# Attention scores from split queries and keys in a hybrid attention and state-space block

## The reference, cut to what matters

```python
h = rms_norm(x, norm_mix_pre[l])
z = h @ w_in[l]                       # q | k | v | u | gates
q = partial_rope(q, pos); k = partial_rope(k, pos)
s = jnp.einsum('bnqhgd,bnkhd->bnhgqk', qb, kb).astype(jnp.float32) / math.sqrt(HEAD_DIM)
s = jnp.where(mask[None, :, None, None], s, jnp.finfo(jnp.float32).min)
p = jax.nn.softmax(jnp.concatenate([s, sink], axis=-1), axis=-1)[..., :-1]
o = jnp.einsum('bnhgqk,bnkhd->bnqhgd', p.astype(v.dtype), vb)
...                                   # state-space branch from u, lam, b_re, b_im, c_re, c_im
mixed = (g_attn * y_attn + g_ssm * y_ssm) @ w_out[l]
x = x + rms_norm(mixed, norm_mix_post[l])
a = jax.nn.relu(rms_norm(x, norm_mlp_pre[l]) @ w_up[l])
x = x + rms_norm((a * a) @ w_down[l], norm_mlp_post[l])
```

## Time and profile before

| | |
|---|---|
| median of 3 runs | 2510.0 us (2509.37 to 2514.89) |
| the profiled execution: its time | 2509.61 us |
| its span, first to last instruction | 2507.6 us |
| PE busy | 2483.1 us, 99% |
| DVE busy | 1281.0 us, 51% |
| ACT busy | 683.4 us, 27% |
| POOL busy | 176.3 us, 7% |
| mean granted TensorE clock | 0.998 of full speed |

### The profile page before, as it was taken

The page is one execution under the profiler, slowest core; times in us unless marked ns, Lnnn a source line. Parts: engine busy times, 40 slices in busy tenths (PEclk is TensorE's granted clock), DMA queues, the critical chain, the costliest instruction groups (busy, mean ns, idle before and its releaser), DMA issues.

```text
span 2507.6 us, 30373 instructions
## 1 busy us (share of the span) xinstructions
PE 2483.1 (99%) x11747; PEld 2027.9 (81%) x11747; DVE 1281.0 (51%) x1622; ACT 683.4 (27%) x903; POOL 176.3 (7%) x284
## 2 busy tenths in 40 slices
PE   9999999999999999999999999999999999999998
PEld 7866887877888888888888888888888888888886
DVE  7876688887434442354444344344334434433446
ACT  5145223333422222252222222212212222121222
POOL 1120243430000000000000000000000000000000
PEclk9999999999999999999999999999999999999999
DMA  6431343443334453343332332223332222333342
GB/s 218 111 105 51 101 123 113 125 125 112 118 101 142 142 181 105 102 163 106 101 101 88 105 100 92 84 100 100 100 100 95 89 94 91 99 100 100 100 153 98
DMA packets 83592, 278.22 MB, mean 111 GB/s; under 512 B 17984, under 2 KB 18048, under 8 KB 81728
## 3 DMA queue, kind: packets, MB, share of 16 engines
q1 hardware_dynamic: 64224, 232.81, 28.9%
q0 software_dynamic: 6624, 27.07, 3.3%
q10 hardware_dynamic: 12672, 17.34, 2.0%
HBM read 258.24 MB, written 18.94 MB: 111 GB/s over the span
## 4 chain that ended last, share of the span: by engine, by line
PE 95%; DVE 2%; ACT 1%; DMA 1%; issue 0%; DVEq 0%; POOL 0%; ACTq 0%
PE main L1568 15%; PE main L1570 14%; PE main L1569 14%; PE side L1764 6%; PE side L1763 6%; PE side L1762 6%; PE main L1763 5%; PE main L1764 5%; PE main L1762 5%; PE side L1568 5%; PE side L1570 5%; PE side L1569 5%; PE side L1626 1%; PE side L1707 1%; PE side L1636 1%; PE side L1676 1%
## 5 line engine op out<-in xcount | busy, mean ns | idle before, releaser
L505 ACT ACTIVATE w_hi<-w_raw 128x1024 fp32r<-128x1024 f32 x436 | 453.7, 1056 | 1080.2 <-PE main L1570 396.4
L880 DVE TENSOR_TENSOR w_lo<-w_raw,w_hi 128x1024 fp32r<-128x1024 f32 x436 | 530.7, 1234 | 361.8 <-ACT w_hi L505 342.5
L1568 PE MATMUL main<-h_hi,w_hi 128*128 128x512 f32 x1280 | 505.4, 395 | 2.5 <-DVE h_lo L896 2.5
L1570 PE MATMUL main<-h_hi,w_lo 128*128 128x512 f32 x1280 | 498.9, 390 | 0.0
L1569 PE MATMUL main<-h_lo,w_hi 128*128 128x512 f32 x1280 | 498.6, 389 | 0.0
L1568 PEld LDWEIGHTS main<-h_hi,w_hi 128*128 128x128 f32 x1280 | 240.6, 188 | 57.3 <-issue 6.6
L1570 PEld LDWEIGHTS main<-h_hi,w_lo 128*128 128x128 f32 x1280 | 240.4, 188 | 50.8
L1569 PEld LDWEIGHTS main<-h_lo,w_hi 128*128 128x128 f32 x1280 | 240.7, 188 | 48.1 <-issue 0.2
L1568 PE MATMUL side<-h_hi,w_hi 128*128 128x512 f32 x512 | 199.2, 389 | 0.0
L1569 PE MATMUL side<-h_lo,w_hi 128*128 128x512 f32 x512 | 199.2, 389 | 0.0
L1570 PE MATMUL side<-h_hi,w_lo 128*128 128x512 f32 x512 | 199.2, 389 | 0.0
(11 more groups left out here) (322 smaller groups left out, 3135.2 us busy)
## 6 DMA issues: line engine op xcount, KB each, us to landing
w_raw<-wstream SPq DMA_DIRECT2D x436, 512.0 KB, 3.6
gate_scratch<-gate_stage ACTq DMA_DIRECT2D x16, 512.0 KB, 3.9
gate_attn<-gate_scratch POOLq DMA_DIRECT2D x8, 512.0 KB, 3.7
gate_ssm<-gate_scratch POOLq DMA_DIRECT2D x8, 512.0 KB, 4.5
x_rows<-x_rows POOLq DMA_DIRECT2D x4, 1024.0 KB, 11.5
x_scratch<-x_rows ACTq DMA_DIRECT2D x4, 1024.0 KB, 4.0
x_all<-x_scratch POOLq DMA_DIRECT2D x4, 1024.0 KB, 8.1
x<-x_t POOLq DMA_DIRECT2D x7, 512.0 KB, 5.9
```

Of the source, the lines that this page charges most:

```text
L505: nc.scalar.activation(WH[:, s], RAW[:, s], ACT.Copy).then_inc(hi_ready, 1)
L880: tt(WL[:, s], RAW[:, s], WH[:, s].bitcast(F32), ALU.subtract).then_inc(lo_ready, 1)
L1568: mm(o, wh, xh[:, k0 + k], start=first and k == 0, stop=False)
L1570: ins = mm(o, wl, xh[:, k0 + k], start=False, stop=last and k == 3)
```

## The change

The scores are made as three products of halves in fp32r, as the units are: high queries by high keys, low queries by high keys, high queries by low keys, all into the same bank. For that ACT writes `q_hi` (four pieces of 128x1024, behind units 12, 13, 16, 20) and `k_hi` (128x512, behind unit 24), and DVE `q_lo` (in the place of the queries, behind units 13, 14, 17, 21) and `k_lo` (behind 24). The halves need 20 KiB a partition more, for which buffers move: NPB falls from 12 to 8, the state inputs `BB`, `BE`, `BT`, `CW` get other homes, and with the homes the points in time at which they may be written. The loads of `BB` wait until `x` has been read, the load of the mask until `b_lo` is done; `rotation(0)` goes behind the last scores; `clear_bw(0)` goes from unit 24 to unit 34 of DVE's list and `load_bw(0)` from unit 26 to unit 35 of ACT's.

```diff
+    QL = at("q_lo", [8, T], 128, F32R)
+    QH = [at(f"q_hi{k}", [4, T], kib, F32R) for k, kib in enumerate((191, 160))]
+    KH = at("k_hi", [T], 180, F32R)
+    KL = at("k_lo", [T], 176, F32R)
-    NPB = 12
+    NPB = 8
...
-            pool.dma_start(MASK[:], consts[:, 1152:1408]).then_inc(consts_landed, 16)
+            pool.wait_ge(xsq_ready, 4)
+            pool.wait_ge(xl_ready, KT)
...
             pool.wait_ge(start_ready, 1)
+            pool.wait_ge(bl_ready, 2)
+            pool.dma_start(MASK[:], consts[:, 1152:1408]).then_inc(mask_landed, 16)
             plink(nc.gpsimd.memset(CBD[:], 0.0))
             load_c(0)
             load_b(0)
-            pool.wait_ge(bl_ready, 2)
-            rotation(0)
             c_by_a(0)
             b_by_state(0)
+            pool.wait_ge(scores_done, 32)
+            rotation(0)
             pool.wait_ge(o_ready, 8)
...
-                if n == 26:
+                if n in (12, 13, 16, 20):
+                    b = (12, 13, 16, 20).index(n)
+                    act.wait_ge(rope_done, b + 1)
+                    t = 2 * b % 4
+                    nc.scalar.activation(QH[b // 2][:, t:t + 2], Q[:, 2 * b:2 * b + 2], ACT.Copy).then_inc(qkh_ready, 1)
+                if n == 24:
+                    act.wait_ge(rope_done, 5)
+                    nc.scalar.activation(KH[:], KTOK[:], ACT.Copy).then_inc(qkh_ready, 1)
+                if n == 35:
                     act.wait_ge(b_stored, 16)
                     load_bw(0)
...
+            def q_lo(b):
+                v.wait_ge(qkh_ready, b + 1)
+                t = 2 * b % 4
+                x = slice(2 * b, 2 * b + 2)
+                link_to(tt(QL[:, x], Q[:, x], QH[b // 2][:, t:t + 2].bitcast(F32), ALU.subtract), qkl_ready, b + 1)
...
-                         20: ((b_bar,),), 21: ((b_even,),), 22: ((b_lo, 0), (b_lo, 1)), 24: ((clear_bw, 0),)}
+                         20: ((b_bar,),), 21: ((b_even,),), 22: ((b_lo, 0), (b_lo, 1)), 24: ((k_lo,),), 34: ((clear_bw, 0),)}
...
-                    for b in range(2):
-                        r = slice(HEAD * b, HEAD * b + HEAD)
-                        ins = mm(side[:, b, first_key(g):2 * P], Q[r, a % 8, n * P:n * P + P],
-                                 KTOK[r, n * P - P + first_key(g):n * P + P], start=True, stop=True)
+                    qh, ql = QH[a % 8 // 4][:, a % 4], QL[:, a % 8]
+                    for i, (q, key) in enumerate(((qh, KH), (ql, KH), (qh, KL))):
+                        for b in range(2):
+                            r = slice(HEAD * b, HEAD * b + HEAD)
+                            ins = mm(side[:, b, first_key(g):2 * P], q[r, n * P:n * P + P],
+                                     key[r, n * P - P + first_key(g):n * P + P], start=i == 0, stop=i == 2)
                     ins.then_inc(scores_done, 1)
...
                 if n == N_SLOT0:
-                    pe.wait_ge(rope_done, 5)
+                    pe.wait_ge(qkl_ready, 5)
```

More of the change, by code:

```diff
@@ L130, in build @@
     KTOK = at("k_t", [T], 176)
-    VTOK = at("v_tok", [TT_N, P], 178.5)
-    MASK = at("mask", [2 * P], 181)
+    VTOK = at("v_tok", [TT_N, P], 178)
+    MASK = at("mask", [2 * P], 182)
     SUM0 = at("square_sum", [4, T], 183)
-    BB = at("b_bar", [CT, 2, SSM_S], 191)
-    BE = at("b_even", [CT, 2, SSM_S], 195)
+    BB = at("b_bar", [CT, 2, SSM_S], 112)
+    BE = at("b_even", [CT, 2, SSM_S], 116)
     tmp = [at(f"param{k}", [4 * ST if k in (8, 9) else ST], 144 + 0.5 * k) for k in range(11)]
     CT4 = at("coef_rows", [P], 150)
-    CW = at("coef_by_channel", [4, NW], 160)
+    CW = at("coef_by_channel", [4, NW], 176)
     BC = at("b_parts", [CT, 2, 2, 2, SSM_S], 144, F32R)
-    BT = [at(f"b_bar_tmp{k}", [CT, SSM_S], 112 + 2 * k) for k in range(2)]
+    BT = [at(f"b_bar_tmp{k}", [CT, SSM_S], 120 + 2 * k) for k in range(2)]
     BSR = at("b_state_raw", [4, 2, 32], 183)
@@ L216, in build @@
         x_first, x_landed = [sem("x_first0"), sem("x_first1")], [sem(f"x_landed{s}") for s in range(4)]
-        cols_landed = sem("cols_landed")
+        cols_landed, mask_landed = sem("cols_landed"), sem("mask_landed")
         consts_landed, small_landed, par_landed, b_landed = (
@@ L225, in build @@
             sem("rope_done"), sem("vt_done"), sem("v_ready"))
+        qkh_ready, qkl_ready = sem("qkh_ready"), sem("qkl_ready")
         angle_ready, trig_ready, bb_ready, b1_ready = (
@@ L1051, in normed, with k_lo @@
                 link_to(tt(out_, pair(b), both(RSTD[:]), ALU.mult), bank_read, b + 1)
+            def q_lo(b):
[3 more added lines that the diff above has]
+                link_to(tt(QL[:, x], Q[:, x], QH[b // 2][:, t:t + 2].bitcast(F32), ALU.subtract), qkl_ready, b + 1)
+            def k_lo():
+                v.wait_ge(qkh_ready, 5)
+                link_to(tt(KL[:], KTOK[:], KH[:].bitcast(F32), ALU.subtract), qkl_ready, 5)
             SWAP = [r ^ 8 if r < ROT else r for r in range(32)]
@@ L1056, in rope_q @@
                 x = Q[:, 2 * b:2 * b + 2]
-                v.wait_ge(consts_landed, 48)
+                v.wait_ge(consts_landed, 32)
                 link(nc.vector.stream_shuffle(KV[:], x, SWAP))
@@ L1156, in _ @@
                     rope_q({11: 0, 12: 1, 15: 2, 19: 3}[n])
+                if n in (13, 14, 17, 21):
+                    q_lo((13, 14, 17, 21).index(n))
                 if n == 21:
@@ L1161, in _ @@
                 if n == N_SLOT0 + 2:
+                    v.wait_ge(mask_landed, 16)
                     v.wait_ge(b_stored, 16)
@@ L1599, in _ @@
                 if n == 13:
-                    pe.wait_ge(consts_landed, 48)
+                    pe.wait_ge(consts_landed, 32)
                     pe.wait_ge(coef_ready, 1)
```

## The result

| | before | after |
|---|---|---|
| median of 22 runs each, taken in turns | 2510.53 us (2507.06 to 2514.89) | 2516.31 us (2510.57 to 2519.12) |
| the profiled execution: its time, its span | 2509.61, 2507.6 us | 2511.15, 2509.4 us |

The ratio is 1.0020, with a 95% interval of 1.0014 to 1.0026: slower by 5.0 us (3.5 to 6.5); the two medians lie 5.8 us apart. The forecast was 2513.5 with a range to 2518; the median is 2.8 us above the forecast and inside the range. The change of 0.2% lies right at the bound that the prediction drew between the same and slower.

A forecast was written before the change was run, and what follows sets the result against it. PE bounds the kernel (busy 99%), in balance with DVE in slots 29 to 31. +0.55 - 0.3 + 1.1 + 2.2 = +3.5 us on 2509.61 gives 2513.1; with 0.4 for the median, 2513.5 us, range 2509.5 to 2518.

The forecast's parts named there:

- the bound that the prediction drew between the same and slower: Whole kernel: within 0.2% (5 us) counts as the same, chance 0.61; slower means above 2515.0, chance 0.35.
- The products of 256 keys: Scores of 24 steps: three fp32r passes hold PE for 0.56 us instead of 0.63, -1.7 us if nothing else held PE.
- The products of 128 keys: Scores of eight steps in slots 24 and 25: 0.50 us instead of 0.42, +0.55 us in all.
- its rival at 2515.9: Slots 24 and 25: each 128-column pass costs 0.21, scores take 0.85, up to 3.4 us in place of 0.55; chance 0.14.
- The sentence on the Trainium skill: Scores of 128 keys: a load costs about 107 ns, three passes at least 0.32 us, eight steps about 0.9 us.
- The eight buffers: Masks 1 and 2 wait for transposes; DVE's loop costs +1.1 us over slots 27 to 31, slot 26 gives -0.3.
- The loads: Slot 33: late clearing and eight loads on ACT's queue delay a copy, PE waits about 2.2 us, +2.2.
- `rotation(0)` costs nothing: POOL: begins with the last scores, wanted only behind the first state products at 277.30, so no cost.
- The clock falls twice: Rival: half clock also behind slot 33's new wait, as behind slot 28's, where it cost 1.7 us; 2515.2; chance 0.21.
- the loads are not in the way: Rival, slot 33: ACT's copies pass the issues or the clearing comes early, 2.2 not paid, 2511.3; chance 0.13.
- slot 28 keeps its clock: Rival, slot 28: the fall to half clock does not come, 1.7 us less, 2511.8; chance 0.09.
- all of the fewer passes is cashed (2507.1): Rival, scores: three fp32r passes against four float32 passes save 2.9 us if no wait grows; chance 0.06.

The follow-up runs named there:

- experiment 4: The changed kernel with 12 probability buffers in place of 8, the third group of four in u's region written last: 2513.09 us, ratio 1.0006.
- experiment 1: The changed kernel with ACT's eight loads of BW moved behind the last four copies of ACT: 2512.29 us, ratio 1.0006.
- experiment 3: The kernel before with only the clearing of BW moved behind unit 34 and its eight loads behind unit 35: 2515.02 us, ratio 1.0015.
- experiment 2: The kernel before with 8 in place of 12 probability buffers and nothing else: 2513.47 us, ratio 1.0011.
- experiment 5: The changed kernel with 12 probability buffers and the loads of BW behind the last copies: 2510.71 us, ratio 1.0000.
- experiment 7: The kernel before with only the scaling of u in slot 28 moved from ahead of mask 0 to behind mask 1: 2507.55 us, ratio 0.9990.

## Why the prediction was nearly right

**The products of 256 keys: right.** 0.55 to 0.56 us, as forecast from the state products.

**The products of 128 keys: right in sign, over-sized.** Forecast +0.55 for slots 24 and 25, measured +0.38. A step takes 0.48 from load to load; I had taken 0.50. The upper bound of 0.21 a pass, and its rival at 2515.9, are out. The sentence on the Trainium skill (TensorE: Matmul & The Clock Gate, section LDWEIGHTS (loading the stationary operand)) had the pace of the passes right and the sum (0.9) too high, because it set three loads of 107 ns against two recorded passes of 0.105 and left the fixed part of 0.21 as it was. By the rows a step grew by 0.055.

**The eight buffers: right.** Slot 26 was forecast at -0.3 and is -0.31; slots 27 to 31 at +1.1 together and are +1.07, at 12.50 to 12.52 with a wait of PE of 0.49 to 0.50 each. The mechanism is on the rows: the mask is released by the transposes, and experiment 4 takes the waits away by giving the buffers back. What the prediction did not put into one figure is that the same four buffers cost 2.98 us against a kernel that keeps twelve, as they also keep the products' saving from being cashed.

**The loads: right.** Forecast +2.2, measured +2.19; experiment 1 takes it away, experiment 3 makes it from the kernel before. The issue took 3.71 us and not 4.16, but the clearing ended 2.85 us behind the slot's start where I had 2.57, and two gaps of 0.1 came in behind it; these nearly cancel.

**Slot 32: the step that was missed.** The sum has nothing for it, and it gave +0.64. The maxima of the last group are later (2.03 us behind the start of slot 32, 1.14 before) and with them the exponentials; the copy for PE is queued behind four of these on ACT. Eight buffers are a part of it, but not alone: in experiment 2, with eight buffers and nothing else, the maxima begin 1.73 us behind the start and slot 32 keeps its 10.25. With the rest of the change and twelve buffers it takes 10.36 to 10.40.

**"`rotation(0)` costs nothing": it has a part in this.** The prediction asked only when its result is wanted, not what it runs beside. It runs from 233.86 to 243.65, beside DVE's last `normalise` and maxima. The `normalise` takes 2.39 us in place of 2.19, and from the end of the reduction (238.37) to the end of `softmax_neg_max` (239.27) DVE takes 0.90 in place of 0.47: together 0.63 us of lateness ahead of the exponentials. So the +0.64 came with both, eight buffers and the late `rotation(0)`: experiment 2 has the first alone and pays nothing in slot 32, experiments 4 and 5 have the second alone and pay 0.11 to 0.15. How the 0.64 divides is not shown, since no run moves `rotation(0)` alone.

**The clock falls twice: a rival that came in part.** The forecast sum was +3.5 with one fall of the clock, and the slots gave +3.98 with one fall. The median of the runs is +5.8, and the 1.8 us between are in no term of the sum; that the median stayed inside the range is owed to the width left for this rival. Experiment 4's profile shows the second fall, at 1.74 us where the rival said 1.7; the profiles of the change and of experiment 3 do not show it in slot 33, with waits of 2.02 and 2.21. So the event that had 0.21 as an alternative exists in some executions and not in others, as the falls behind slot 36 do. The runs' mean clocks, on record to three decimals each, say how much half clock there was: 0.9965 in the 22 runs of the change, 0.9971 with the loads behind (experiment 1), 0.9963 in experiment 3, 0.9969 in the 60 runs of the kernel before that lie beside the experiments. One stretch of 3.4 us at half clock takes 0.5 x 3.4 / 2509 = 0.0007 off such a mean. So late loads go with about 0.9 of a stretch more a run, with and without the other edits (in both pairs within 0.7 either way, 95%). At 1.5 to 1.7 us each that is the size of what the change and experiment 3 lose in the median beyond their slots (1.8 and 1.5 us). That these stretches lie in slot 33 is argued: the runs' clocks don't say where they fell, and experiment 4, whose profile had the fall, has a median 0.8 below its slots.

The runs of the change also fall apart into four up to 2511.28 and 18 from 2514.10 on. Slot 33 alone does not explain such a gap: the profiled run of experiment 3 lies 4.0 us above the shortest of its 11 runs, and its clock fell twice behind slot 36 and not in slot 33.

**The other rivals.** That the loads are not in the way, that slot 28 keeps its clock (it fell there in all seven profiles that keep the wait) and that all of the fewer passes is cashed (2507.1) did not come. The last is answered by experiments 5 and 7: even with no wait in its way, the saving of the products is 0.9 to 1.2 us in the slots, of the 2.9 that counting passes gives.

## What to carry to other kernels

When memory is freed for a change, price the buffers given up first: ask for each user of the ring which event now frees its buffer, and follow the lateness to the end of the loop and one stage past it. Loads issued from a compute engine's queue hold up all that is written behind them there, 0.46 to 0.52 us apiece here; put them where that queue idles, or behind the copies that TensorE waits for. And look at the longest single wait before counting passes: one 1.2 us operation of DVE moved behind a mask was worth three times what the new products were, in the slots (2.98 and 0.94 us).

## What the runs showed of the hardware that was not expected

- **The same wait lowers the clock in one execution and not in another.** A wait of 1.81 to 1.83 us near 1100 us, the same code in all nine profiles, was followed by half clock in four; one of 3.28 us near 2480 in four; of the waits in slot 33, 2.02 (the change), 2.21 (experiment 3) and 2.16 us (experiment 4), only the last was; a wait in slot 5 in three (2.66, 2.33 and 2.67 us, experiments 1, 2 and 5) and not in two (2.22 and 2.00, before and experiment 3). Behind slot 28's waits of 2.20 to 2.81 us it fell in all seven profiles that have such a wait; behind waits of 0.94 to 1.22 us (slots 5, 27 and 28) it did not. So the length of the wait alone does not decide it. The half-speed stretch was 3.4 us long each time while PE worked, but 6.8 us once, in experiment 2, at a wait of 2.64.
- **Short passes.** Passes of 128 columns in fp32r on two row tiles follow at 0.10 to 0.11 us, passes of 256 at 0.12. Making the moving side half as long saves almost nothing.
- **DVE and POOL are slower beside each other.** With `rotation(0)` on POOL, the two small operations of DVE at 238.40 and 238.80 take 0.36 and 0.39 us (0.17 each in the kernel before), a `w_lo` 1.80 (1.22 to 1.23 in its neighbours), and an operation of POOL of 128x256 at 241.36 takes 1.60 where its neighbour of the same shape takes 0.73. In experiment 5 a POOL operation of 128x512 takes 2.02 beside DVE's `w_lo` (1.30), and the one ahead of it, beside DVE's `normed`, only 1.04: not every pair that overlaps is slower. `w_lo` has both inputs in SBUF, the `normed` has one of its two in a PSUM bank. What the two engines share was not tested. The Trainium skill (GPSIMD Engine Reference, section 1. Specifications) says that GpSimd and VectorE share their interfaces to SBUF and contend where a VectorE instruction has two inputs from there or runs in a mode with two ports; `w_lo` and `normed` agree with the first of these. `softmax_neg_max`, with one input, took 0.44 in experiments 4 and 5 in place of 0.16; whether it ran in such a mode, no view here shows.
